# Decoder trunk in fp32r pairs: the first norm's token factor moved from the first projection's operand to its results

## The reference

```python
def _even_mixer(h, w_in, a_conv, b_conv, b_conv_bias, b_ln_g, b_ln_b, w_out):
    p = h @ w_in                                     # 2048 -> 7 * 1024
    a_x, a_b, a_c, a_z, b_val, b_gate, b_z = jnp.split(p, 7, axis=-1)
    ya = a_b * _causal_dwconv(a_c * a_x, a_conv)     # 3 taps
    yb = b_val * jax.nn.sigmoid(b_gate)
    yb = _causal_dwconv(yb, b_conv) + b_conv_bias    # 31 taps
    yb = jax.nn.silu(_layernorm(yb, b_ln_g, b_ln_b))
    u = jnp.concatenate([ya * jax.nn.silu(a_z), yb * jax.nn.silu(b_z)], axis=-1)
    return u @ w_out

h = _rmsnorm(x, e_norm_pre[i])    # x * rsqrt(mean(x*x) + eps) * gain
x = x + _rmsnorm(_even_mixer(h, ...), e_norm_post[i])
```

## Time and profile before

| | |
|---|---|
| Median of 3 runs | 1379.74 us (1379.19 to 1381.48) |
| Profiled execution, span on the core | 1378.9 us |
| TensorE busy | 1340.4 us (97%), 6274 matmuls |
| VectorE busy | 861.3 us (62%) |
| ScalarE busy | 451.2 us (33%) |
| GpSimd busy | 109.6 us (8%) |
| Moved by DMA | 171.69 MB |

### The profile page before, as it was taken

The page is one execution under the profiler, slowest core; times in us unless marked ns, Lnnn a source line. Parts: engine busy times, 40 slices in busy tenths (PEclk is TensorE's granted clock), DMA queues, the critical chain, the costliest instruction groups (busy, mean ns, idle before and its releaser), DMA issues.

```text
span 1378.9 us, 15711 instructions
## 1 busy us (share of the span) xinstructions
PE 1340.4 (97%) x6274; PEld 1124.6 (82%) x6274; DVE 861.3 (62%) x805; ACT 451.2 (33%) x445; POOL 109.6 (8%) x102
## 2 busy tenths in 40 slices
PE   5999999999999999999999889999999999999997
PEld 4988888888888888888888679888888888788885
DVE  7588888888763323334987985444532222499788
ACT  5331332232222211224555452222222222445552
POOL 5100000000005400000000100000000001410001
PEclk9999999999999999999999999999999999999999
DMA  8233434343343333362604674433333332355157
GB/s 249 62 93 92 121 91 122 91 115 91 98 122 92 91 92 92 92 213 75 230 31 140 249 228 117 124 100 106 96 91 91 98 115 92 119 191 179 40 201 248
DMA packets 223657, 171.69 MB, mean 125 GB/s; under 512 B 2944, under 2 KB 195584, under 8 KB 222208
## 3 DMA queue, kind: packets, MB, share of 16 engines
q1 hardware_dynamic: 219248, 165.86, 39.5%
q10 hardware_dynamic: 4368, 5.24, 1.1%
HBM read 162.71 MB, written 8.39 MB: 124 GB/s over the span
## 4 chain that ended last, share of the span: by engine, by line
PE 90%; DVE 6%; ACT 1%; DMA 1%; issue 1%; POOL 0%; SPq 0%; DVEq 0%; ACTq 0%
PE bank L594 30%; PE bank L596 30%; PE bank L598 30%; DVE w_lo L1413 1%; DVE scratch L1442 1%; DVE h_lo L1295 1%; DMA rows<-x_t 1%; DMA scratch<-o_out 0%; PE bank L630 0%; ACT w_hi L977 0%; DVE rows L1288 0%; DMA scratch<-e_out 0%; DVE raw L1442 0%; DVE scratch L1301 0%; ACT h_hi L971 0%
## 5 line engine op out<-in xcount | busy, mean ns | idle before, releaser
L594 PE MATMUL bank<-h_hi,w_hi 128*128 128x512 f32 (+1 forms) x1600 | 598.9, 374 | 10.1 <-DVE w_lo L1240 4.9
L596 PE MATMUL bank<-h_lo,w_hi 128*128 128x512 f32 (+1 forms) x1600 | 596.6, 373 | 0.0
L598 PE MATMUL bank<-h_hi,w_lo 128*128 128x512 f32 (+1 forms) x1600 | 596.5, 373 | 0.0
L594 PEld LDWEIGHTS bank<-h_hi,w_hi 128*128 128x128 f32 x1600 | 302.8, 189 | 65.0 <-DVE w_lo L1240 5.4
L598 PEld LDWEIGHTS bank<-h_hi,w_lo 128*128 128x128 f32 x1600 | 302.7, 189 | 52.7
L596 PEld LDWEIGHTS bank<-h_lo,w_hi 128*128 128x128 f32 x1600 | 302.8, 189 | 52.3 <-issue 0.5
L1240 DVE TENSOR_TENSOR w_lo<-raw,w_hi 128x2048 fp32r<-128x2048 f32 x89 | 207.0, 2326 | 53.9 <-ACT w_hi L871 47.0
L1328 DVE SCALAR_TENSOR_TENSOR rows<-shifted,vecs,rows 128x512 f32 x256 | 198.0, 776 | 42.2 <-ACT rows L931 10.9
L871 ACT ACTIVATE w_hi<-raw 128x2048 fp32r<-128x2048 f32 x90 | 171.9, 1910 | 78.3 <-PE bank L598 64.9
L594 PE MATMUL bank<-w_hi,h_hi 128*128 128x512 f32 x448 | 175.9, 393 | 7.7 <-DVE rows L1478 7.7
L596 PE MATMUL bank<-w_lo,h_hi 128*128 128x512 f32 x448 | 175.1, 391 | 0.0
(11 more groups left out here) (113 smaller groups left out, 737.2 us busy)
## 6 DMA issues: line engine op xcount, KB each, us to landing
raw<-e_in SPq DMA_DIRECT2D x54, 1024.0 KB, 5.6
raw<-o_in SPq DMA_DIRECT2D x32, 1024.0 KB, 6.2
spare<-e_out SPq DMA_DIRECT2D x12, 1024.0 KB, 7.3
spare<-o_out SPq DMA_DIRECT2D x12, 1024.0 KB, 7.3
scratch<-e_out SPq DMA_DIRECT2D x10, 1024.0 KB, 5.1
scratch<-o_out SPq DMA_DIRECT2D x10, 1024.0 KB, 5.1
rows<-x_t SPq DMA_DIRECT2D x8, 512.0 KB, 6.8
x_mid<-rows ACTq DMA_DIRECT2D x8, 512.0 KB, 3.6
```

The lines of the kernel that those rows point to most:

```text
L594: nc.tensor.matmul(dst, w[0], m[0], start=first, stop=False, skip_group_check=goes_on)
L596: nc.tensor.matmul(dst, w[0], m[1], start=False, stop=False, skip_group_check=goes_on)
L598: return nc.tensor.matmul(dst, w[1], m[0], start=False, stop=last, skip_group_check=goes_on)
```

## The change

The operand of the first projection is now x times gain alone. The factor per token, r, is put on the results. Since r is one number per token and the taps mix tokens, it must be on `glu` and `prod` before the taps: b_gate and b_val are multiplied by r, and a_c by r squared, which carries the factor of a_x too. In `E1B` and `E1C` the tiles and the gates get r before the silu.

```diff
@@ semaphores, pools of banks
+        x_sums = sb("x_sums", [P, TT])
+        x_tok = [scratch[:, n * T:n * T + D] for n in (2 * TT, 3 * TT)]
+        def first_bank(c):
+            return 4 if c == 0 else 0
@@ SyncE
-            load_x(0)
...
+            sp.dma_start(vecs[:, :], vec).then_inc(vec_loaded, 16)
             for j in range(4):
+                load_x(2 * j)
                 for n in range(RAW):
+                    load_first(n, j)
+                load_x(2 * j + 1)
+            for n in range(RAW):
+                for j in range(4):
+                    if j < 3:
+                        sp.wait_ge(first_lo, RAW * j + n + 1)
+                    else:
+                        sp.wait_ge(lo_ready, n + 1)
+                    load_first(RAW + n, j)
+            for t in range(2):
+                load_tokens(t)
+            for q, kind in enumerate(E1A_ORDER):
+                load(q, columns(e_in, P + kind), SLOTS + q)
+                if q < 2:
+                    sp.wait_ge(x_squared, q + 1)
+                    load_tokens(2 + q)
@@ TensorE: x_sums, half_product, half_slab and x_ready are gone
+            keep_warm(12)
+            for q in range(SLOTS):
+                pe.wait_ge(bank_free[4 + q], 1)
             for k in range(KT):
+                pe.wait_ge(x_lo_ready, k + 1)
                 for q in range(RAW):
+                    first_product(q, k)
             for q in range(RAW, SLOTS):
+                for k in range(KT):
+                    first_product(q, k)
+            def x_spread_out(q, k):
+                if (q, k) == (0, QUARTER):
+                    pe.wait_ge(diagonals_ready, TT)
+                    nc.tensor.matmul(bank[R_BANK][:, :], ones[:, :], diagonals[:, :, :],
+                                     start=True, stop=True).then_inc(x_spread, 1)
+                elif (q, k) == (R_BANK, 0):
+                    pe.wait_ge(x_rstd_ready, 1)
+            feature_major(1, operand, before=x_spread_out)
+            with pe.Fori(2, E1A) as i:
+                feature_major(i, operand)
@@ ScalarE
+            def x_rounded(k):
+                nc.scalar.activation(h_hi[:, k, :], rows[:, k, :], ACT.Identity, bias=0.0,
+                                     scale=col("pre", k)).then_inc(x_hi_ready, 1)
...
+            x_square(0)
+            x_square(1)
+            split_ahead(0, 1)
+            x_square(2)
+            x_square(3)
+            split_ahead(0, 2)
+            split_ahead(0, 3)
+            for c in range(E1A):
...
+                act.wait_ge(bank_free[first], first_used(c))
+                nc.scalar.activation(sig, sig, ACT.Sigmoid).then_inc(sig_ready, 1)
@@ VectorE
+            def x_rest(k):
+                dve.wait_ge(x_hi_ready, k + 1)
+                nc.vector.scalar_tensor_tensor(
+                    out=h_lo[:, k, :], in0=rows[:, k, :], scalar=col("pre", k),
+                    in1=f32(h_hi[:, k, :]), op0=ALU.mult, op1=ALU.subtract)\
+                    .then_inc(x_lo_ready, 1)
...
+            split_ahead(0, 1)
+            dve.wait_ge(x_squared, TT)
+            nc.vector.tensor_scalar(token_var[:, :], x_sums[:, :], 1.0 / D, EPS,
+                                    ALU.mult, ALU.add).then_inc(x_var_ready, 1)
+            split_ahead(0, 2)
+            dve.wait_ge(x_power_ready, 1)
+            dve.wait_ge(consts_set, 6)
+            make_diagonals()
+            split_ahead(0, 3)
+            dve.wait_ge(x_spread, 1)
+            link(nc.vector.tensor_copy(x_rstd, bank[R_BANK][:, :]))
+            nc.vector.tensor_tensor(x_rstd2, x_rstd, x_rstd, ALU.mult).then_inc(x_rstd_ready, 1)
...
-            with dve.Fori(0, E1A) as c:
+            for c in range(E1A):
+                if c > 0:
+                    split_ahead(c, 1)
+                nc.vector.tensor_tensor(sig, bank[first][:, :], x_rstd, ALU.mult)\
+                    .then_inc(bank_free[first], 1)
-                nc.vector.tensor_tensor(glu[:, PAD:], bank[1][:, :], sig, ALU.mult)\
-                    .then_inc(bank_free[1], 1)
+                nc.vector.tensor_tensor(glu[:, PAD:], bank[first + 1][:, :], x_rstd, ALU.mult)\
+                    .then_inc(bank_free[first + 1], 1)
+                dve.wait_ge(sig_ready, c + 1)
+                nc.vector.tensor_tensor(glu[:, PAD:], glu[:, PAD:], sig, ALU.mult)\
+                    .then_inc(glu_ready, 1)
...
+                nc.vector.tensor_tensor(a_c, bank[first + 2][:, :], x_rstd2, ALU.mult)\
+                    .then_inc(bank_free[first + 2], 1)
+                convolve(c, conv_done, glu, CONV_B, "conv_b", 21, 23)
...
-                convolve(c, conv_done, glu, CONV_B, "conv_b", 21, 25)
+                convolve(c, conv_done, glu, CONV_B, "conv_b", 23, 25)
                 split_ahead(c + 1, 0)
+            def scaled(q, step, n, buf):
+                dve.wait_ge(slab_done, done(step * SLOTS + (q + 1)))
+                dve.wait_ge(gated, n + 1)
+                nc.vector.tensor_tensor(sz[buf], bank[q][:, :], x_rstd, ALU.mult)\
+                    .then_inc(bank_free[q], 1)
```

424 lines of the change are left out of this document (150 added, 274 removed).

## The result

| | before | after |
|---|---|---|
| Median in this comparison | 1380.46 us (1379.19 to 1381.48) | 1357.66 us (1356.19 to 1360.51) |
| Ratio | | 0.9839, 95% interval 0.9827 to 0.9851 |
| Profiled execution, its own time | not recorded | 1356.8 us |
| Its span | 1378.9 us | 1355.0 us |

The account below looks back on a forecast made before the run. TensorE, busy in 97% of the span, was taken to bound the kernel. The terms -13.1 - 8.2 + 0.9 + 1.8 = -18.6 us gave a span of 1360.3 and a time of 1361.1 us, range 1356.5 to 1369.5.

Parts of the forecast that it names:

- Bound: Whole kernel: TensorE busy in 97% of the span; only its idle time and its own instructions' price can move the time.
- Term 1: Start: first projection matmul no longer waits for the token factor, at 9.3 us in place of 22.42: -13.1 us.
- Term 2: Step 0 of the first projection: 192 matmuls with 512 columns, fed in time, 46.1 in place of 54.3 us: -8.2 us.
- the clock: Step 0: first matmuls at TensorE's lower level cost 2.6 us; the small matmuls ahead end too early to help.
- Term 3: Spreading matmul now stands within step 1 and pushes the matmuls behind it: +0.9 us.
- Term 4: Step 1: late factor starts VectorE's pass 0 6.0 us in, against a deadline of 4.2: +1.8 us, once.
- The pass: VectorE's pass over a channel block takes 41.0 us, under TensorE's step of 43.5, so lateness is not passed on.
- Costed at nothing: Steps 9 to 13 and last gate: VectorE's added multiplications are covered by its idle time, 7.4 us before a gate.
- A: VectorE sets the pace: written-out waits gain nothing on taps, a pass takes 44.2 us; 1369 us, chance 0.12.
- B: Factor very late: pass 0 starts 12 us into step 1, 8 us of stall; 1367 us, chance 0.08.
- C: TensorE's clock doesn't rise in step 0 because of repeated short stops; 1378 us, no change, chance 0.04.
- D: Slower than before: VectorE's passes above 46.4 us eat the start's gain; at 47 us a pass 1389 us, chance 0.03.

Follow-up runs that it names:

- the early table: Kernel after, with one 128 x 1 activation on a constant run on ScalarE before its wait for x: 1356.58 us, ratio 0.9828.
- the second of the delayed kernels: Kernel after, with twelve chained unused copies of 128 x 512 on VectorE between the token factor and its square: 1366.16 us, one time.
- the second profile of the kernel after: Kernel after, unchanged, measured once more beside two candidates: 1358.18 us, ratio 0.9843.
- the first delayed kernel: Kernel after, with six chained unused copies of 128 x 512 on VectorE between the token factor and its square: 1361.67 us, one time.

## Why the prediction held, point by point

**Bound.** Right: TensorE's idle time and its own matmuls were the only two things that moved. Its sum of 18.6 us stands against 22.0 at the column-sum matmul, and 22.8 between the medians. Moving the factor and the new order of the loads of x and weights were measured together: no run separates what each has of terms 1 and 2.

**Term 1, the start: 12.2 in place of 13.1 us.** The step that failed is the chain from the landing of weights to the first matmul: it had no table load. Before, that load ran from 0.83 on, ahead of x; in the change it stands behind the landing of x, and measured 1.28 us. With the load early the first matmul moved from 4.29 to 2.99 us behind x. A second error hid part of it, and that was luck: the forecast let the first matmul wait for the second weight quarter (landing at 7.5), but it needs only the first. With the early table it stands at 7.73, before that quarter is even rounded (7.91), and the matmul on the second quarter stands at 9.32, just where the forecast had the first. Within a microsecond the term also depends on when x lands: 4.67 to 5.97 us in twelve profiles.

**Term 2, step 0: 10.7 in place of 8.2 us.** The mechanism was right (192 whole columns, 43.6 us, fed without a stop). The part mis-sized is the clock, put at 2.6 us. The upper bound of the prediction, 2.85 us for a cold start, fits the 2.5 us measured without the small matmuls. What failed is "the twelve small matmuls end several us too early to help": they ran until 8.0 us, since at the lower clock each was two records of 0.229 us, and the pause was 2.3 us. The part is 0 or 1.6 us by the execution, so that the first profile, with 0, was in part lucky. Nine profiles have the twelve small matmuls and the wait for x of about the same length: behind pauses of 0.8 to 1.7 us none shows the lower clock in step 0, behind pauses of 2.1 to 2.3 us four of five do. The pause alone doesn't decide it, as the two courses behind 1.77 us in one kernel show. The 2.6 us for whole columns were right: 2.5 measured.

**Term 3, spreading: 0.9 us,** as forecast (22.9 less 22.0).

**Term 4, the late factor: 0 in place of 1.8 us.** Both sides were off. The first multiplication stood 5.2 us into step 1, not 6.0. The deadlines are 6.7 and 6.0 us, not 4.9 and 4.2: pass 0 takes 26.7 us from its first multiplication to the end of slab 7's remainder (59.10 to 85.78), not 27.6, and the 0.86 us that the spreading adds to the step were costed in term 3 but not given to VectorE as time. With the deadlines right and its own start of 6.0, the term would have been 0.

**The pass: 40.3 in place of 41.0 us.** Taps 0.787 (forecast 0.785). The head was 3.1 and not 3.9: of the added 1.8 us 1.05 came, since the sigmoid runs beside the second multiplication and leaves 0.17 us of idle time behind it. `hi` after `prod` cost 1.2 of the 1.3.

**Costed at nothing.** VectorE is still idle 5.4 us before a gate (7.4 before), and the output projection starts with the same 1.98 us of VectorE's idle time. Both held.

**The rivals.** A (0.12) would have come without the written-out waits: pass 44.0 us measured, 44.2 forecast, though at 5.2 to 5.7 us on top in place of 8. B (0.08) has its measure in the second of the delayed kernels: a factor 5.5 us later against the step costs 5.7 us, 1.6 of it clock. C (0.04) did not occur, though step 0 has pauses: 0.66 us in one profile didn't lower the clock. (The stops at `h_lo` that the prediction holds against C lie at 27 to 35 us in the kernel before, and they are four; the fifth of the earlier trace rows is the one at 22.42, ahead of the rise.) D needed a pass of 46.4 us and was never near. The Trainium skill (TensorE: Matmul & The Clock Gate, HAM oscillation) describes waits of 3 to 5 us for transfers, behind which each short group of matmuls starts at the lower clock. Behind all stops of 3.1 to 4.9 us the traces agree with it, but step 0 has no stop of that length.

**Left over.** At the column-sum matmul the forecast is 3.4 us too cautious (22.0 against 18.6), which the terms account for: 2.5 + 1.8 - 0.9 = 3.4. The spans differ by 1.9 us more, the medians by 0.8. From the column-sum matmul to the end the profiles have 953.9 us before and 952.1 after, but 953.0 in the second profile of the kernel after and 952.7 in the kernel before with its loops written out. In the profiles the waits for `rows` behind 700 us fell from 7.7 us (four) to 6.7 (three), but they vary from 5.0 to 7.4 among the kernels made from the kernel after. So neither is put down to the change. The step from the span to the time was also mis-sized: the prediction added 0.8 us, a distance between the span of one execution and the median of others, while in each profiled execution that has both, the time is 1.8 us above the span.

## What to carry to other kernels

A factor that commutes with a product needn't stand ahead of it; put on the results it takes its whole chain off the start, and what is left to check is a deadline: at which time the first consumer's products are wanted, counted in the consumer's own steps. An engine in the shadow of another can pay for added work, but only with the spare time per step, so a cheaper form of its inner instruction (a wait on a constant, 0.1 us a tap) decides whether the change is a gain, although the same edit alone measures as nothing. Where an engine's first instruction stands behind a wait, a one-element activation ahead of that wait takes the table load off the path; any wait added in front of an activation with another table has to be looked at in the same way.

## What the runs showed of the hardware

- **A pause costs more than itself.** Behind 3.81 us of idle time the matmuls stood 0.427 us apart for 3.4 us: 1.6 us on top. Behind 4.78 and 4.93 us TensorE ran at the lower level too, for 3.0 and 3.8 us in the kernel after. After 1.77 us at 755.8 us it did not happen, but after 1.77 us at 754.7 us in a second execution of the same kernel it did, 1.3 us behind the pause. After 1.98 us in the first delayed kernel it didn't, after 1.80 us at 793.7 us in another it did, 0.8 us behind the pause. So pauses near 2 us go either way, and in one kernel from one execution to the next. The loss counts only where TensorE is the bound: at 793 us it was hidden.
- **At the start the granted clock reads 1.00** even where matmuls stand 0.427 us apart (10 to 14 us in the kernel without the small matmuls). There the distances tell the level, and the column doesn't.
- **A copy of 128 x 512 from SBUF to SBUF on VectorE** took 0.457 us in a chain, the like from a bank 0.69 us.
